# Input tiles of their own for two feed-forward stages, at other byte offsets

## The reference

```
def swiglu(x, w_gu, w_down):
    gate, up = jnp.split(x @ w_gu, 2, axis=-1)
    return (jax.nn.silu(gate) * up) @ w_down

x = x + 0.5 * rms_norm(swiglu(rms_norm(x, ffn1_pre_g[l]), ffn1_w_gu[l], ffn1_w_down[l]), ffn1_post_g[l])
...
x = x + 0.5 * rms_norm(swiglu(rms_norm(x, ffn2_pre_g[l]), ffn2_w_gu[l], ffn2_w_down[l]), ffn2_post_g[l])
```

## Time and profile before

| | us |
|---|---|
| median of 3 runs | 1642.7 |
| the runs | 1640.82, 1642.7, 1647.88 |
| the profiled execution, its time | 1648.82 |
| its span | 1647.2 |
| TensorE busy with matmuls | 1525.4 |
| VectorE busy | 1086.4 |
| ScalarE busy | 727.8 |
| GpSimd busy | 309.5 |

### The profile page before, as it was taken

One profiled execution on the slowest core, in us unless ns is written; L12 is line 12 of the kernel. 1 busy time (PEld: TensorE's weight loads), 2 busy tenths in 40 slices (PEclk: granted clock), 3 DMA queues, 4 the chain that ended last, 5 costly groups with the idle time before them and its releaser, 6 DMA issues.

```text
span 1647.2 us, 27694 instructions
## 1 busy us (share of the span) xinstructions
PE 1525.4 (93%) x10710; PEld 1399.8 (85%) x10710; DVE 1086.4 (66%) x1590; ACT 727.8 (44%) x835; POOL 309.5 (19%) x306
## 2 busy tenths in 40 slices
PE   5998889899999999998999999998999897789997
PEld 5987679799999999997888888888998795589976
DVE  5644466579899988945555555567774575577743
ACT  4335554344545445434444444444443357244431
POOL 2000000000010011114667676630000010000000
PEclk8999889999999999999999999999999996789999
DMA  6552224447676578886888888864555440245551
GB/s 239 193 185 91 78 72 157 147 169 250 209 245 231 175 274 277 280 285 242 293 287 295 287 288 291 283 239 141 203 182 178 177 167 26 90 143 202 201 174 60
DMA packets 56290, 329.65 MB, mean 200 GB/s; under 512 B 7472, under 2 KB 7520, under 8 KB 24720
## 3 DMA queue, kind: packets, MB, share of 16 engines
q1 hardware_dynamic: 35856, 259.01, 45.0%
q0 software_dynamic: 20352, 69.47, 12.3%
HBM read 294.90 MB, written 33.55 MB: 199 GB/s over the span
## 4 chain that ended last, share of the span: by engine, by line
PE 82%; DVE 10%; ACT 4%; issue 2%; DMA 2%; DVEq 0%; SPq 0%; ACTq 0%
PE ub L1506 14%; PE ub L1508 14%; PE ub L1507 14%; PE acc L1506 11%; PE acc L1507 11%; PE acc L1508 11%; DVE wl L861 3%; PE acc L1693 3%; DMA raw<-in_wstream 1%; ACT wh L526 1%; PE acc L1571 1%; PE acc L1470 1%; PE ub L1595 0%; DVE esel L1205 0%; DVE nw_b L877 0%
## 5 line engine op out<-in xcount | busy, mean ns | idle before, releaser
L861 DVE TENSOR_TENSOR wl<-raw,wh 128x2048 fp32r<-128x2048 f32 x245 | 568.6, 2322 | 293.9 <-ACT wh L526 292.7
L1506 PE MATMUL ub<-xh,wh 128*128 128x256 f32 x2216 | 627.9, 283 | 19.9 <-DVE wl L861 7.2
L1507 PE MATMUL ub<-xl,wh 128*128 128x256 f32 x2216 | 621.6, 280 | 0.0
L1508 PE MATMUL ub<-xh,wl 128*128 128x256 f32 x2216 | 621.5, 280 | 0.0
L526 ACT CAST wh<-raw 128x2048 fp32r<-128x2048 f32 x245 | 467.3, 1908 | 257.5 <-DMA raw<-in_wstream 124.7
L1506 PEld LDWEIGHTS ub<-xh,wh 128*128 128x128 f32 x2216 | 424.2, 191 | 23.5 <-DVE wl L861 21.6
L1508 PEld LDWEIGHTS ub<-xh,wl 128*128 128x128 f32 x2216 | 425.0, 192 | 0.0
L1507 PEld LDWEIGHTS ub<-xl,wh 128*128 128x128 f32 x2216 | 424.9, 192 | 0.1
L1506 PE MATMUL acc<-wh,ah 128*128 128x512 f32 x512 | 200.0, 391 | 8.1 <-issue 8.1
L1507 PE MATMUL acc<-wl,ah 128*128 128x512 f32 x512 | 199.8, 390 | 0.0
L1508 PE MATMUL acc<-wh,al 128*128 128x512 f32 x512 | 199.6, 390 | 0.0
(11 more groups left out here) (315 smaller groups left out, 1655.3 us busy)
## 6 DMA issues: line engine op xcount, KB each, us to landing
raw<-in_wstream SPq DMA_DIRECT2D x245, 1024.0 KB, 4.9
gates<-gst POOLq DMA_DIRECT2D x16, 1024.0 KB, 14.8
gl_in<-gates POOLq DMA_DIRECT2D x64, 256.0 KB, 3.2
hidden<-hid POOLq DMA_DIRECT2D x60, 256.0 KB, 4.6
hid<-hidden POOLq DMA_DIRECT2D x60, 256.0 KB, 3.0
resid<-in_x SPq DMA_DIRECT2D x2, 512.0 KB, 4.0
rb<-in_rel POOLq DMA_DIRECT2D x1, 1024.0 KB, 11.0
wb<-in_ffn_post_g POOLq DMA_DIRECT2D x2, 512.0 KB, 3.9
```

The source lines that it names most:

```text
L861: v.tensor_tensor(wl[:, slot, :], raw[:, slot % RAW, :], wh[:, slot, :].bitcast(F32), ALU.subtract).then_inc(w_low, 1)
L1506: pe.matmul(dst, sh, mh, start=first, stop=False)
L1507: pe.matmul(dst, sh, ml, start=False, stop=False)
L1508: return pe.matmul(dst, sl, mh, start=False, stop=last)
```

## The change

Both feed-forward layers get a pair of input tiles of their own, in one allocation `fx` behind `fg`. `tiles_of` gives views of it: for the first layer from the start of `fx`, for the second 48 elements (192 bytes) further. With 56 elements of filler before it, `fx` begins 96 bytes off a multiple of 256, and the second layer's tiles begin 32 bytes off one (96 + 192 = 256 + 32). The low tile lies 2112 elements, 8448 bytes or 33 x 256, behind the high one, so it has the same offset. The views replace `xh` and `xl` as the target of `normed` and the source of the `gu` chunks. Everything else goes on with `xh` and `xl`.

```diff
         fg = sb("fg", [P, 2, 2, T], at=st1)
+        sb("shift_f", [P, 56], at=st1)
+        fx = sb("fx", [P, 2, KD * T + 64], F32R, at=st1)
...
+        def tiles_of(gu):
+
+            at = {"gu1": 0, "gu2": 48}[gu]
+            return [fx[:, k, at:at + KD * T].rearrange("p (k t) -> p k t", t=T) for k in range(2)]
...
-            def normed(w, u):
+            def normed(w, u, dst=xh):
...
-                    act.activation(xh[:, k, :], turned(k, u), ACT.Copy,
+                    act.activation(dst[:, k, :], turned(k, u), ACT.Copy,
...
-                normed(w, UN[gu])
+                normed(w, UN[gu], tiles_of(gu)[0])
...
-            def normed(w, u):
+            def normed(w, u, dh=xh, dl=xl):
...
-                    v.scalar_tensor_tensor(xl[:, k, :], turned(k, u),
-                                           wcol[:, w, k:k + 1], xh[:, k, :].bitcast(F32),
+                    v.scalar_tensor_tensor(dl[:, k, :], turned(k, u),
+                                           wcol[:, w, k:k + 1], dh[:, k, :].bitcast(F32),
...
-                normed(w, UN[gu])
+                normed(w, UN[gu], *tiles_of(gu))
...
-            def unit_chunk(c, cmod, u, umod, tiles=2, fresh=False):
+            def unit_chunk(c, cmod, u, umod, tiles=2, fresh=False, sh=xh, sl=xl):
                 pe.wait_ge(w_low, c + 1)
-                unit(cmod % RING, u, umod % 2, tiles=tiles, fresh=fresh).then_inc(c_done, 1)
+                unit(cmod % RING, u, umod % 2, tiles=tiles, fresh=fresh, sh=sh, sl=sl).then_inc(c_done, 1)
...
+                fxh, fxl = tiles_of(gu)
                 for j in range(2):
-                    unit_chunk(C + j, C + j, U + j, U + j, fresh=j == 0)
+                    unit_chunk(C + j, C + j, U + j, U + j, fresh=j == 0, sh=fxh, sl=fxl)
...
-                        unit_chunk(i * 4 + (C + j), C + j, i * 4 + (U + j), U + j)
+                        unit_chunk(i * 4 + (C + j), C + j, i * 4 + (U + j), U + j, sh=fxh, sl=fxl)
```

## The result

The changed kernel took 1653.88 us (median of 4 runs, 1653.2 to 1659.18), the kernel before 1642.35 us (4 runs, 1640.82 to 1647.88): a ratio of 1.0071, 95% interval 1.0040 to 1.0102. The forecast was no change, 1643 us in a range of 1635 to 1653; it was slower by 11.5 us, just outside.

What follows compares the result with a forecast made beforehand. TensorE, never idle in the two stages, was taken as the bound, through matmul count and pace. All terms were 0: 1648.8 us profiled + 0, or 1642.7 against the median, rounded 1643 us; range 1635 to 1653.

Steps and rivals of the forecast that it cites:

- the term of the moving operand: In the 2112 `gu` matmuls of both stages, moving rows at new offsets keep the quick pace of 113.3 ns: cost 0.
- its 232.9 ns: Pace with `xh` stationary, 2.8% above 226.5 ns with `ah`; offset or two-valued pace, not separated by the rows.
- The upper bound: On the `gu` matmuls' loss: the slow pace, 118.0 against 113.3 ns, 5.0 us a stage, 9.9 us for both.
- a sign of being wrong: A pace at an odd multiple of 32 bytes that is neither of the two seen, 113.3 and 118.0 ns.
- The forecast of no change: Both feed-forward stages keep 113.3 ns a matmul, time 1643 us; chance of the same time 0.74.
- Rival B: One or both `gu` stages fall to the slow pace: 1648 us for one (chance 0.12), 1653 for both or worse (0.14).
- the writes, the waits or the instruction count: In both stages: no instruction or wait added, cost 0; the 16 writes a stage cost 0, at most 0.1 us.
- The loss reached the end of the stages whole: In both stages, other engines having room, a gain or a loss would reach the end whole.
- The stages before the first feed-forward layer: Stages before 1120 us read nothing that moved; if they differ, the difference is not the change's.
- Rival C: New offsets remove 6.6 ns a `gu` matmul: 1629 us whole, 1636 half; chance 0.08 in part, 0.10 near whole.
- The Trainium skill's rule: TensorE reads moving and stationary operands through independent ports and waits for nobody, so the moving operand's term is 0.

Runs made afterwards that it cites:

- the second measurement: The changed kernel unaltered, run with more rounds against the kernel before: 1654.1 us (6 runs) against 1646.51 us (11 runs), ratio 1.0048.
- the kernel with 128 and 0: The changed kernel with first-stage tiles 128 bytes off a multiple of 256 and second-stage tiles 0 off: 1654.22 us, one run.

## Why the prediction was wrong

**The step that failed** is the term of the moving operand, "I take 0: over the offsets that can be seen the quick pace does not depend on where the moving operand begins". It measured 5.1 and 5.4 ns a matmul, 5.4 + 5.7 = 11.1 us by the windows and 10.7 us by the chain. The offsets that could be seen were 64 for `xh` and 128 for the weights, but the second was the moving operand of the other form, whose stationary operand is also 128 off. I read two points of a pair as if they were two points of one number. The runs show a relation between the two operands: 64 below is quick in the 128 x 256 form, 0 is quick in the 128 x 512 form and costs 120.0 ns in the other. The form is part of the relation, so one form's good offset says nothing of the other's.

The prediction left open whether its 232.9 ns, with `xh` stationary in the 128 x 512 form, came from the offset or from a two-valued pace. The traces show both. From start to start these matmuls at 284 us stand 228.9 ns apart in 6 of the 14 profiled executions and 233.3 ns in the other 8, and never at the 226.7 ns that `ah` has in all of them.

**The upper bound** was taken from the slow pace of `xh`, 118.0 ns, 9.9 us for both stages. Both stages stood a little above it, and other offsets reach 120.1 ns, (120.1 - 113.3) x 2112 = 14.4 us. A pace seen at the old offset bounds no other offset; that 118.4 and 118.7 are neither of the two paces seen is what the prediction itself named as a sign of being wrong. The result lies only 0.9 us outside the range, and a difference of 7.6 us, as the second measurement has it, would have been within the 10 us that the range allows above the forecast; on which side of the bound it fell was luck. The forecast of no change fails in both: neither interval reaches 1. Rival B had the mechanism, the counts ("about 850 and 281 ns") and nearly the time (1653) right, with a chance of 0.14.

**What held.** No cost from the writes, the waits or the instruction count: with the tiles at 64 in the new place the ratio is 0.9997. The loss reached the end of the stages whole, 10.7 us by the chain, as no other engine was near its limit. The stages before the first feed-forward layer kept their paces. Rival C, that the excess over the column count can be had back, found no support: none of the eleven offsets went below 113.3 ns.

**The Trainium skill's rule** that TensorE's two reads are independent and wait for nobody (page "SBUF — State Buffer", section "Who interferes with whom") spoke for 0. The runs contradict it as a rule of pace: 32 bytes in the stationary reads alone moved a stage from 118.4 to 113.7 ns and another from 113.3 to 120.0.

**What stays open.** That the two reads meet in the memory is the plain reading of this, but no run shows the memory, only the two addresses. What picks one of the paces at the same addresses was not tried, nor why the same distance of 96 below has three of them. No version here beats the kernel before; its tiles already were at the only good offset found.

## What to carry to other kernels

Where TensorE goes without a gap, count matmuls in a window for each stage and compare the paces before trusting that a tile may lie anywhere: here up to 6% of a stage hung on 8 bytes. Judge an operand's offset by the distance to the other operand of the same matmul, modulo 256 bytes (the low tile in `fx` lies 33 x 256 bytes behind the high one and was as quick; 128 bytes further, at 192, was slow), in the same form and shape, and keep that distance when a tile is added, since a new tile in an allocation moves all that follow. If a tile needs a place of its own, give it the offset of the one that it replaces first and measure others afterwards.

## What the runs showed of the hardware

The kernel's own spread has a visible part of the same kind. The stretch from 346 to 436 us reads `xh` at the same addresses relative to the weights in all kernels here. In 8 of the 14 profiled executions, the one before and the one after among them, it held 765 to 767 matmuls (118 ns by the window, 117.8 from start to start), in the other 6 it held 796 or more (113.3 ns). The stretch at 446 us was slow in one, the kernel with 128 and 0 (639 in 75 us against 664):

```profile
346.00:436.00 90.00, 90.00 (x797) 1.00 0.66 225
446.00:521.00 75.00, 75.00 (x639) 1.00 0.68 232
```

A pace once entered is kept for tens of us. The slow stretch of the kernel before in three parts:

```profile
346.00:376.00 30.00, 30.00 (x256) 1.00 0.53 176
376.00:406.00 30.00, 30.00 (x257) 1.00 0.74 251
406.00:436.00 30.00, 30.00 (x257) 1.00 0.64 215
```

One such stretch is worth 816 x 4.7 ns = 3.8 us. That would be a good part of the 7 us between the fastest and the slowest run of the kernel before, though which pace the runs without a profile had is not known; a difference of 0.2% between two single runs of it says nothing. No feed-forward stage with the good distance was caught in the slow pace, in 8 stages of four kernels, the kernel before among them. Eight are too few to say that none ever is: the mixer's input product reads `xh` at the same distance and was slow in two of the 14, both kernels with filler ahead of all tiles. This is the second of them, 173 matmuls where the kernel before has 179:

```profile
1330.00:1350.00 20.00, 20.00 (x173) 1.00 0.55 193
```
